# A state-space group norm: how the squares are summed, and where in TensorE's queue it happens

## The reference

```python
def rms_norm(x, g):
    y = x32 * lax.rsqrt(jnp.mean(x32 * x32, axis=-1, keepdims=True) + NORM_EPS)
    return (y * g).astype(x.dtype)

y = ssd_chunked(xs, dt, a, bm, cm) + d_skip * xs
y = y * silu(z)
y = rms_norm(y.reshape(bsz, s, SSM_GROUPS, D_INNER // SSM_GROUPS), g_ssm_norm)
y_ssm = y.reshape(bsz, s, D_INNER) @ w_ssm_branch
```

## Time and profile before

| | |
|---|---|
| median of 3 runs | 1263.46 us (1263.16 to 1264.37) |
| profiled execution | 1261.9 us, span 1260.0 us |
| TensorE matmuls busy | 1240.6 us, 98% of the span |
| VectorE busy | 761.9 us, 60% |
| ScalarE busy | 581.6 us, 46% |
| GpSimd busy | 406.2 us, 32% |
| granted TensorE clock, mean | 0.998 of full speed |

### The profile page before, as it was taken

How to read it: one execution, slowest core, us unless ns; L and a number is a source line. 1 busy time by engine, 2 the same in 40 slices (tenths; PEclk the granted TensorE clock), 3 DMA queues, 4 the chain that set the end, 5 groups by cost and what they waited for, 6 DMA issues and landing times.

```text
span 1260.0 us, 19071 instructions
## 1 busy us (share of the span) xinstructions
PE 1240.6 (98%) x6684; PEld 1020.5 (81%) x6684; DVE 761.9 (60%) x1352; ACT 581.6 (46%) x1012; POOL 406.2 (32%) x271
## 2 busy tenths in 40 slices
PE   9999999999999999999999999999999999999997
PEld 7888877777888888888888888888878888888885
DVE  6845887775577877787764111121158749479387
ACT  6315566666544554454442222222366346354364
POOL 3433355545333333333334444444420110301200
PEclk9999999999999999999999999999999999999999
DMA  8533310000222222222222333334452160430601
GB/s 246 160 87 70 80 37 2 1 2 2 68 83 68 77 73 67 72 78 79 70 67 84 100 100 93 91 99 158 126 193 74 34 211 22 141 125 17 215 2 67
DMA packets 170327, 108.39 MB, mean 86 GB/s; under 512 B 25284, under 2 KB 161830, under 8 KB 170278
## 3 DMA queue, kind: packets, MB, share of 16 engines
q1 hardware_dynamic: 170038, 107.65, 29.3%
q10 hardware_dynamic: 240, 0.09, 0.0%
HBM read 104.84 MB, written 2.10 MB: 85 GB/s over the span
## 4 chain that ended last, share of the span: by engine, by line
PE 87%; DVE 4%; ACT 4%; issue 2%; POOL 1%; DMA 1%; SPq 0%; DVEq 0%; ACTq 0%; POOLq 0%
PE bank L2459 21%; PE bank L2055 16%; PE bank L2468 10%; PE bank L2059 8%; PE bank L2563 8%; PE bank L2568 4%; PE bank L2303 2%; PE bank L2478 2%; PE bank L2243 2%; PE bank L2282 2%; POOL prob L865 1%; PE bank L2104 1%; PE bank L2143 1%; PE bank L2484 1%; PE bank L2439 1%
## 5 line engine op out<-in xcount | busy, mean ns | idle before, releaser
L845 POOL TENSOR_TENSOR wlo<-raw,whi 128x1024 fp32r<-128x1024 f32 x133 | 324.3, 2438 | 687.5 <-ACT whi L1091 384.9
L1091 ACT ACTIVATE whi<-raw 128x1024 fp32r<-128x1024 f32 x96 | 101.8, 1060 | 291.9 <-PE bank L2468 159.5
L2055 PE MATMUL bank<-h_hi,whi 128*128 128x512 f32 x456 | 181.6, 398 | 0.7 <-DVE h_lo L1332 0.7
L2055 PE MATMUL bank<-h_lo,whi 128*128 128x512 f32 x456 | 178.0, 390 | 0.0
L2459 PE MATMUL bank<-h_hi,whi 128*128 128x512 f32 x384 | 150.3, 391 | 1.3 <-DVE grp L1775 0.7
L2459 PE MATMUL bank<-h_lo,whi 128*128 128x512 f32 x384 | 149.5, 389 | 0.0
L2059 PE MATMUL bank<-h_hi,wlo 128*128 128x512 f32 x456 | 112.9, 390 | 0.0
L1863 DVE TENSOR_TENSOR mt<-bank,sig 128x512 f32<-128x512 f32 x16 | 11.1, 691 | 161.6 <-PE bank L2468 161.6
L1755 DVE SCALAR_TENSOR_TENSOR grp<-bank,vt,grp 128x511 f32<-128x511 f32 (+2 forms) x96 | 71.8, 748 | 58.7 <-ACT grp L1115 49.8
L865 POOL TENSOR_SCALAR prob<-prob,rsum,gate 128x512 f32<-128x512 f32 (+3 forms) x128 | 79.4, 634 | 80.4 <-DVE rsum L1599 80.4
L2055 PEld LDWEIGHTS bank<-h_hi,whi 128*128 128x128 f32 x456 | 85.7, 188 | 20.0 <-DVE h_lo L1332 2.5
(11 more groups left out here) (321 smaller groups left out, 2538.5 us busy)
## 6 DMA issues: line engine op xcount, KB each, us to landing
raw<-in_w_in SPq DMA_DIRECT2D x71, 512.0 KB, 3.8
raw<-in_w_up SPq DMA_DIRECT2D x32, 512.0 KB, 4.1
draw<-in_w_down SPq DMA_DIRECT2D x16, 1024.0 KB, 6.5
raw<-in_w_ssm_branch SPq DMA_DIRECT2D x16, 512.0 KB, 3.7
raw<-in_w_in SPq DMA_DIRECT2D x28, 256.0 KB, 3.3
raw<-in_w_attn_branch SPq DMA_DIRECT2D x8, 512.0 KB, 3.7
raw<-in_w_o SPq DMA_DIRECT2D x8, 512.0 KB, 3.7
x_sb<-in_x SPq DMA_DIRECT2D x4, 512.0 KB, 5.1
```

The lines of the kernel that those rows point to most:

```text
L845: nc.gpsimd.tensor_tensor(wlo[slot][:], raw[slot][:], whi[slot][:].bitcast(F32), ALU.subtract).then_inc(wlo_ready, units)
L1091: nc.scalar.activation(whi[slot][:], raw[slot][:], ACT.Copy).then_inc(whi_ready, 1)
L2055: T.matmul(bank[slot][:], whi[slot][:, k * P:(k + 1) * P], part[:, k, :], start=(k == 0 and n == 0), stop=False)
```

## The change

`norm_sum` transposes the four chunks of `sq` into bank 5, so that tokens lie on partitions and channels along the free axis. VectorE then sums each chunk's 128 values with one reduction from the bank into a new tile `y_mean`, and the first small instruction multiplies by 1/256 and adds EPS. `mean_ssm` and its memset go, which lowers by one the counts of `ones_set` that engines wait for. In the loop's groups, `norm_sum` is issued inside unit 3, behind its first four matmuls; `norm_spread` stays behind the segment sum of unit 3. On VectorE `conv(2)` now stands ahead of `norm_root`. In `mix` the places stay.

```diff
@@ norm_root, VectorE
-                mean, part, corr = (bank[sums][:, i * NC:(i + 1) * NC] for i in range(3))
+                part, corr = (bank[sums][:, i * NC:(i + 1) * NC] for i in range(2))
+                mean = y_mean[:]
                 dve.wait_ge(yms_done, g + 1)
                 root_step = Steps(dve, root_steps)
-                root_step.base = g * 10
-                root_step(V.tensor_scalar(mean, mean, EPS, None, ALU.add))
+                root_step.base = g * 11
+                root_step(V.tensor_reduce(mean, bank[sums][:].rearrange("p (c n) -> p c n", c=NC), AX.X, ALU.add))
+                root_step.wait()
+                root_step(V.tensor_scalar(mean, mean, GROUPS / D_INNER, EPS, ALU.mult, ALU.add))
@@ group, VectorE
                 silu(0)
+                conv(2)
                 if not first:
                     norm_root(g - 1)
-                conv(2)
                 silu(1)
@@ unit, TensorE
-            def unit(u, slot, read=None, landing=None, units=1):
+            def unit(u, slot, read=None, landing=None, units=1, inside=None):
...
+                    if inside is not None and k == 1:
+                        inside()
@@ norm_sum, TensorE
-                    mm = T.matmul(bank[sums][:, c:c + 1], sq[:, c * P:(c + 1) * P], mean_ssm[:, 0:1], start=True, stop=True)
+                    mm = T.transpose(bank[sums][:, c * P:(c + 1) * P], sq[:, c * P:(c + 1) * P], ident)
@@ group, TensorE
+                def last_norm_sum():
+                    norm_sum(g - 1)
+
                 for j in range(1, 4):
-                    group_unit(j)
+                    group_unit(j, inside=last_norm_sum if j == 3 and not first else None)
                     seg(j)
-                    if j == 2 and not first:
-                        norm_sum(g - 1)
-                    elif j == 3 and not first:
-                        norm_spread(g - 1)
+                if not first:
+                    norm_spread(g - 1)
                 group_unit(4)
@@ GpSimd's start
-            nc.gpsimd.memset(mean_ssm[:], GROUPS / D_INNER).then_inc(ones_set, 1)
```

More of the change, by code:

```diff
@@ L165, in build @@
         ones = sb("ones", [P, P])
-        mean_ssm = sb("mean_ssm", [P, P])
         ident_bf = sb("ident_bf", [P, P], BF16)
@@ L176, in build @@
         root = sb("root", [P, NC])
+        y_mean = sb("y_mean", [P, NC])
         decay_rows = sb("decay_rows", [P, S], F32R)
@@ L706, in swap_rows @@
                 if n == 0:
-                    sp.wait_ge(ones_set, 5)
+                    sp.wait_ge(ones_set, 4)
                 for row in (0, 8, HD, HD + 8):
@@ L898, in _ @@
             assert at_row == VEC_ROWS
-            act.wait_ge(ones_set, 3)
+            act.wait_ge(ones_set, 2)
             nc.scalar.activation(stat[:, 4:5], eps_col[:, 0:1], ACT.Sqrt)
@@ L1689, in norm_root @@
                         ins.then_inc(yrs_ready, 1)
-                assert root_step.n == 10
+                assert root_step.n == 11
             def normed_y(g, spread=5):
@@ L2090, in turn_dt @@
                 pe.wait_ge(a_spread, 1)
-                pe.wait_ge(ones_set, 3)
+                pe.wait_ge(ones_set, 2)
                 for c in range(NC):
@@ L2370, in group, with group_unit @@
             def group(g, first):
-                def group_unit(j):
+                def group_unit(j, inside=None):
                     if j < 2:
@@ L2376, in group_unit @@
                         pe.wait_ge(conv_summed, g * 4 + (j - 1))
-                    unit(g * 6 + (U_SSM + j), j % 2)
+                    unit(g * 6 + (U_SSM + j), j % 2, inside=inside)
                 def seg(c):
```

## The result

The changed kernel took 1269.55 us, median of 6 runs (1268.69 to 1271.69), against 1263.49 for the kernel before (1263.16 to 1264.37). The ratio is 1.0051, 95% interval 1.0041 to 1.0061: 6.1 us slower by the medians. The sign was forecast, the size (3.2 us) was half of it, and the time lies 0.55 us above the range. The profiled execution took 1270.06 us with a span of 1268.2.

A forecast was written before the change was run, and what follows sets the result against it. TensorE, busy for 98% of the span, was taken as the bound. Seven loop groups at 0.40 us (2.8) plus 0.4 in mix gave 3.2, added to the median 1263.46: 1266.7 us, range 1262.5 to 1269.0.

The forecast's parts named there:

- TensorE's queue: Loop groups: norm_sum's 1.28 us removed, four transposes at 0.45 added, so 0.83 us shorter a group without any new wait.
- The chain of the root: Loop, first tap through conv(2), reduction and root steps to TensorE's load: 6.34 us, ending at 421.46 in group 2.
- The stall: TensorE reaches norm_spread at 420.26, the root is there at 421.46: a wait of 1.20 us in group 2.
- the net: Unit 4 starts about 0.40 us later in each of the loop's seven groups, 2.8 us in all.
- The overlap at conv's end: VectorE's next independent instruction, the reduction, starts 0.08 us before conv(2) ends.
- The cover: Loop: the root is ready 3.4 us before TensorE comes to norm_spread; the change spends this.
- The last group: In mix, where TensorE already waits 0.27 us for the root: 0.37 to 0.47 us later, taken as 0.42.
- The bounds: Limits of the unknown costs: groups lose 0.34 us each at best, 0.7 at worst, so up to 1269 us.
- rival B: Gain and stall cancel through a chain 0.1 to 0.7 us shorter a group: about 1264.5 us, chance 0.25.
- What I costed at nothing: Earlier conv(2), later silu(1), conv(3)'s thin cover, the memset, semaphore counts, DMA and bank 5: no time added.
- A: Rival: the root on VectorE isn't late and TensorE keeps its shorter queue: 6.3 us less, 1257.2, chance 0.12.
- C: Rival: silu(1) and conv(3) late for transposes behind unit 4, 0.2 to 0.3 us in seven groups: 1268.5, chance 0.12.

The follow-up runs named there:

- Experiment 3: Changed kernel with the mean in PSUM, loop spread behind six matmuls of unit 4, mix spread behind fourteen matmuls: 1256.28 us against 1262.20, ratio 0.9947.
- experiment 1: Changed kernel with the mean kept in PSUM in place of the new SBUF tile: 1266.18 us against 1262.20, ratio 1.0028.
- experiment 2: Changed kernel with norm_spread in the loop moved inside unit 4, behind its first six matmuls: 1260.94 us against 1262.20, ratio 0.9981.
- experiment 4: Kernel before, with the mean in an SBUF tile in the first pass of mix alone: 1267.06 us against 1262.20, ratio 1.0031.
- Experiment 7: Changed kernel's transposes and reduction at the old places and in the old order, mean in the SBUF tile: 1278.80 us, ratio 1.0133.
- experiment 10: Changed kernel, mean in the SBUF tile, with the spreads in the loop and in mix both moved later: 1259.19 us against 1262.74, ratio 0.9974.
- experiment 5: Kernel before, unchanged, run once more for a second profile: 1264.09 us, beside a median of 1263.40.
- experiment 6: Changed kernel's transposes and reduction at the old places and in the old order, mean in PSUM: 1263.49 us against 1263.40, ratio 1.0001.

## Why the prediction was wrong, and where it was right

**TensorE's queue.** Right. 0.83 us less a group was forecast before any wait. Experiment 3, which has the shorter queue and no waits, comes out 6.7 us below the kernel before, for 6.3 by the sum.

**The chain of the root.** Right in every term, and shown to be the only loss in the loop: from the first tap to TensorE's load the sum gave 6.34 us and the trace has 6.32 (416.62 to 422.94). The stall was forecast with 1.20 us and is 1.17 (1.01 on the matmul row, 1.45 on the load row), the net with 0.40 a group and 2.8 in all, measured 0.41 in group 2 and 2.7 in all. The overlap at conv's end is there too: the reduction starts at 419.98, and conv ends at 417.52 + 2.54 = 420.06. The prediction took this overlap to disagree with the Trainium skill ("VectorE: DVE Perf Modes", section "The DRAIN you can't avoid"). That section also says that a next operation that is not held starts earlier, so by its whole text there is no disagreement. Moving the spread behind six matmuls removes the loss, behind two brings it back in part, and the order alone does nothing. The cover that the prediction named at the outset, 3.4 us, was spent in three parts as it said: `conv(2)` first, the reduction, TensorE's earlier arrival.

**The last group.** This is the step that failed: "That is 0.37 to 0.47; I take 0.42." It measured 2.6 us, and 1.6 more in the profile for the clock. Under it lies the sentence "The scaling by 1/256 shares the instruction that added EPS, so the eleven small steps stay eleven: 2.21." Eleven they stayed, but three kinds of them lost their PSUM input: the scaling, the seed, and the product of mean and root. In the kernel before each of the eleven read at least one input from PSUM. The bounds took up the reduction, the landing, the overlap and the restart, and the change of operand place only as something that might make the steps quicker (rival B). The experiments show the cause: with the mean in PSUM no step is long, and the term comes out at 0.35 us in experiment 1; with it in SBUF the first such step that meets GpSimd's low-part instruction lasts until that ends, in five kernels (the changed one and experiments 2, 4, 7 and 10) of different order and operations.

The Trainium skill ("SBUF — State Buffer", section "Who interferes with whom") states the rule that was missed: VectorE and GpSimd share one pair of SBUF ports as an exclusive lock, taken by the scalar and copy forms in their two-port modes, and by products of two SBUF inputs against a GpSimd instruction that reads SBUF; who comes first holds it for the whole instruction. The traces can't show the ports themselves, but they agree for both kinds: the scaling took 2.38, 1.91 and 2.40 us in the changed kernel and in experiments 7 and 10, the product 2.37 in experiment 4. The delay could have been priced ahead of time. In the kernel before, the root steps in mix went from 666.45 to 668.63, and GpSimd's row there is:

```profile
666.80 2.40 POOL L845 TENSOR_TENSOR wlo<-raw,whi 128x1024 fp32r<-128x1024 f32 x1 [4.38 <-ACT whi L1091]
```

By the prediction's own terms the scaling would start at 666.45 - 0.35 + 0.72 = 666.82, which is 0.02 us behind GpSimd's start, as it did in the changed kernel.

The forecast missed its range by 0.55 us only, but that nearness is not to its credit: the width of the range was made of costs that did not grow, and the cost that did was in none of its bounds.

**The loop did not show it** because there `conv(2)` and the reduction push the small steps behind GpSimd's instruction: it ends at 419.2 in the changed kernel, and the first small step starts at 420.69. Experiment 7 undoes this and has the delay seven times.

**The clock.** The prediction had no term for it. A wait of 2.0 to 2.9 us in mix was followed by a stretch of lower clock in the profiles of the changed kernel and of experiment 4 (granted clock 0.66 and 0.64 in the stretches shown), but not in those of experiments 2, 7 and 10. In none of the seven profiles without such a wait did the clock fall in mix, but it fell at other places in some, near 165 us in experiment 5 and near 925 us in four profiles. The fall in mix costs 1.6 us in the two profiles that have it. What decides it was not found, and that the wait brings it about is likely and not shown.

**What I costed at nothing.** No wait appeared behind unit 4. That nothing changes at the start is not settled: the profile is 1.2 us late by 60 us (experiment 5). Of the rivals, A named the gain rightly (6.3 us) but not a way to it; C was wrong for this kernel, though its mechanism is just what experiment 6 ran into.

## What to carry to other kernels

When a change moves a small operand from PSUM to SBUF, list every later instruction that then has only SBUF inputs, and look in the trace for what GpSimd does at that time; 128x4 elements can cost 2.4 us. When TensorE is the bound and its queue gets shorter, it comes earlier to each wait that follows: measure how long each result has lain ready, and move the consumer by that much (here behind six matmuls of the next unit) before counting the gain. A cover found idle on the engine where one looks may be needed by the list of a third engine, as ScalarE's in experiment 6.

## What was not expected of the hardware

A VectorE instruction with all its inputs in SBUF that meets a running GpSimd one is shown as busy, not as waiting: 2.38 us of "busy" on 512 numbers, with no idle time in front of it. And a late wait can be followed by a loss half as large again through the clock: at the lower level the matmuls in mix started 0.40 us apart in place of 0.23, and the runs of experiment 2 split into two heaps 1.5 us apart.
